# Two token tiles without indexer queries, a turned order of the norm, and weight halves and requests in other places

## What is computed

```python
z = rms_norm(x, g) @ w_in                     # columns split among all heads
qi = rotary(heads(parts[3], 8, 64), pos)      # indexer queries, 512 columns
ki = rotary(heads(parts[4], 1, 64), pos)      # indexer key, 64 columns
wi = parts[5]                                 # 8 head weights
sc = einsum('bqh,bqhs->bqs', wi * IDX_SCALE, relu(einsum('bqhd,bsd->bqhs', qi, ki)))
sc = where(key_pos <= qpos, sc, -inf)
_, sel = top_k(sc, 256)                       # keys that mixer A attends to
```

## Time and profile before

| | us |
|---|---|
| median of 3 runs | 2079.43 |
| lowest and highest run | 2074.18, 2079.83 |
| span of the profiled execution, first to last instruction | 2075.8 |
| TensorE busy in the span | 1955.8 (94%) |
| VectorE, ScalarE, GpSimd busy | 1279.8, 711.6, 682.9 |

### The profile page before, as it was taken

One profiled execution on the slowest core, in us unless ns is written; L12 is line 12 of the kernel. 1 busy time (PEld: TensorE's weight loads), 2 busy tenths in 40 slices (PEclk: granted clock), 3 DMA queues, 4 the chain that ended last, 5 costly groups with the idle time before them and its releaser, 6 DMA issues. The chain is left out here.

```text
span 2075.8 us, 35829 instructions
## 1 busy us (share of the span) xinstructions
PE 1955.8 (94%) x13869; PEld 1778.6 (86%) x13869; DVE 1279.8 (62%) x2449; ACT 711.6 (34%) x1454; POOL 682.9 (33%) x780
## 2 busy tenths in 40 slices
PE   6889999999998897997899988999999999999997
PEld 6867788899997796554599987999999999999997
DVE  5038999997886355443474235786667676643535
ACT  5234322211212473443322145732323232322423
POOL 5757757678890132553300200301010000301000
PEclk9999999999999999999899999899999999999999
DMA  5122232247665633210473020145454532635334
GB/s 171 32 65 74 74 106 86 94 142 229 219 193 168 232 100 95 60 39 27 148 216 110 22 86 28 33 137 184 143 173 139 187 108 77 225 98 175 121 90 139
DMA packets 203741, 251.41 MB, mean 121 GB/s; under 512 B 29172, under 2 KB 184212, under 8 KB 203060
## 3 DMA queue, kind: packets, MB, share of 16 engines
q1 hardware_dynamic: 170980, 167.53, 26.9%
q0 software_dynamic: 9552, 54.95, 7.5%
q10 hardware_dynamic: 23040, 26.63, 3.6%
HBM read 202.38 MB, written 74.00 MB: 133 GB/s over the span
## 5 line engine op out<-in xcount | busy, mean ns | idle before, releaser
L1122 PE MATMUL pz<-w_hi,n_hi 128*128 128x384 f32 (+2 forms) x656 | 225.1, 343 | 3.8 <-DVE n_lo L909 3.6
L1122 PE MATMUL pz<-w_hi,n_lo 128*128 128x384 f32 (+2 forms) x656 | 219.0, 334 | 0.0
L1122 PE MATMUL pz<-w_lo,n_hi 128*128 128x384 f32 (+2 forms) x656 | 218.8, 334 | 0.0
L966 DVE MATCH_REPLACE8 sel<-m,sel 128x1024 f32<-128x1024 f32 (+4 forms) x224 | 205.4, 922 | 0.0
L963 DVE MAX8 m<-sel 128x8 f32<-128x1024 f32 (+4 forms) x224 | 197.6, 925 | 0.1
L3896 PE MATMUL p_c<-n_t_hi,blk 128*128 128x264 f32 x1120 | 191.3, 285 | 1.8 <-DVE blk L3613 1.8
L3896 PEld LDWEIGHTS p_c<-n_t_hi,blk 128*128 128x128 f32 x1120 | 159.0, 188 | 2.0 <-issue 2.0
L1122 PEld LDWEIGHTS pz<-w_hi,n_hi 128*128 128x128 f32 x656 | 126.6, 193 | 23.9 <-issue 18.4
L3896 PE MATMUL p_c<-mix_hi,blk 128*128 128x264 f32 x816 | 141.1, 285 | 0.0
L1128 PE MATMUL pz<-n_hi,w_hi 128*128 128x352 f32 x384 | 126.6, 330 | 5.1 <-ACT z L614 5.1
L3486 POOL DMA_DIRECT2D g_s<-gate x22 | 12.2, 556 | 358.2 <-DVE gate L3701 333.9
(11 more groups left out here) (520 smaller groups left out, 5124.4 us busy)
## 6 DMA issues: line engine op xcount, KB each, us to landing
shared<-in_w_in SPq DMA_DIRECT2D x26, 768.0 KB, 4.7
blk_raw<-in_w_ffn_in SPq DMA_DIRECT2D x72, 256.0 KB, 3.1
relu<-z_qb SPq DMA_DIRECT2D x24, 512.0 KB, 4.9
blk_raw<-in_w_ffn_out SPq DMA_DIRECT2D x58, 192.0 KB, 2.5
z_b<-z ACTq DMA_DIRECT2D x48, 192.0 KB, 1.9
gates<-z ACTq DMA_DIRECT2D x48, 176.0 KB, 2.8
gate<-gates SPq DMA_DIRECT2D x24, 352.0 KB, 3.5
out_new_win_sample<-in_cache_win_kv POOLq DMA_DIRECT2D x8, 1016.0 KB, 5.7
```

Of the source, the lines that this page charges most:

```text
L966: dve.match_replace(out=sel[0:r, o:o + n], in_to_replace=m8[0:r, u, :], in_values=sel[0:r, o:o + n], imm_value=PICKED).then_inc(s_rep, 1)
L1122: m = pe.matmul(out, tokens(a, k, i), b[:, n % 2, k, 0:w], start=(k == 0 and p == 0), stop=(k == KC - 1 and p == 2))
```

## The change

- **Tiles 0 and 1 have no indexer queries.** `UNPICKED` is 2. Block 0 has no step for them (seven steps are left: tiles 2 to 8), and in block 1 their steps compute columns 256 to 328 alone, the key and the head weights (`FIRST_COL`); evacuation, rotation and transpose are narrowed with them.
- **The order of tiles in the norm and in blocks 0 and 1** is 2 to 8, 0, 1 (`X_ORDER`). The rows are loaded, normed and transposed in this order. The first two steps of block 1 (tiles 2 and 3) stand in the loop of the nine head positions and wait there for the high and low part of the eighth and ninth position, which are tiles 0 and 1 (`if s < TILES`). The sample's step has 32 output rows in place of 128.
- **Low halves.** VectorE makes (1, 1) behind its last `normed`, and (2, 0) and (2, 1) behind its last `lo_norm`. GpSimd's (n + 1, 1) of later blocks stands ahead of the seventh rotation of a block in place of the one of tile 6, which is one step earlier from block 2 on.
- **Requests.** SyncE requests (3, 0) and (3, 1) ahead of the sample rows.

```diff
+UNPICKED = TOPK // P
+X_ORDER = list(range(UNPICKED, TILES)) + list(range(UNPICKED))
 for _n in range(len(PROJ)):
-    for _i in range(TILES):
-        if _i < NT or _n < FOLD_FROM:
+    for _k, _i in enumerate(X_ORDER if _n < FOLD_FROM else range(TILES)):
+        if (_i < NT or _n < FOLD_FROM) and (_n or _i >= UNPICKED):
             STEPS.append((_n, _i, None))
-        if _i == FOLD_BEHIND and FOLD_FROM <= _n + 1 < len(PROJ):
+        if _k == FOLD_BEHIND and FOLD_FROM <= _n + 1 < len(PROJ):
             STEPS.append((_n + 1, NT, None))
...
+FIRST_COL = {s: 256 for s, st in enumerate(STEPS) if st[0] == 1 and st[1] < UNPICKED}
...
-        def lows_by_pool(f):
-            return f - (f > 1)
+        low_by_vector = (1, 3, 4, 5)
+
+        def wait_lows(engine, f):
+            by_vector = sum(x < f for x in low_by_vector)
+            if f - by_vector:
+                engine.wait_ge(s_wlo, f - by_vector)
+            if by_vector:
+                engine.wait_ge(s_wlow, by_vector)
...
                 for b in range(2):
                     load_pages(sp, b)
 
+                for j in range(2):
+                    load_half(3, j)
                 last = FIRST_STEP[NIDX] - 1
...
-                for j in range(2):
-                    load_half(3, j)
...
-                    act.activation(z[:, u, 0:w], pz[:, v, 0:w], ACT.Copy).then_inc(s_zev, 1)
+                    c = FIRST_COL.get(s, 0)
+                    act.activation(z[:, u, c:w], pz[:, v, c:w], ACT.Copy).then_inc(s_zev, 1)
...
                 for s in range(FIRST_STEP[len(PROJ)]):
-                    n, i, _ = STEPS[s]
-                    if i == 3:
-                        split_lo(n + 1, 0)
-                    if i == 6:
-                        split_lo(n + 1, 1)
+                    n = BLOCK_OF[s]
+                    k = s - FIRST_STEP[n]
+                    for j in range(2):
+                        if k == (3, 6)[j] and 2 * (n + 1) + j not in low_by_vector:
+                            split_lo(n + 1, j)
                     rotate(s)
...
                 for i in range(1, TILES):
                     lo_norm(i)
                     if i + 2 < TILES:
                         mean(i + 2)
                         normed(i + 2)
+                    if i == 6:
+                        split_lo(1, 1)
+                split_lo(2, 0)
+                split_lo(2, 1)
...
-                    if n == 0:
-                        pe.wait_ge(s_nhi, i + 1)
-                        pe.wait_ge(s_nlo, i + 1)
+                    if s < TILES:
+                        pe.wait_ge(s_nhi, s + 1)
+                        pe.wait_ge(s_nlo, s + 1)
...
-                        out = pz[:, c % 2, 0:w]
+                        c0 = FIRST_COL.get(s, 0)
+                        out = pz[0:rows(i)[1], c % 2, c0:w]
...
-                    for c in range(2 + n):
+                    for c in range(FIRST_COL.get(s, 0) // P, 2 + n):
```

More of the change, by code:

```diff
@@ L373, in rows, with x_place @@
             return (i * P, NS if i == NT else P)
+        def x_place(p):
+            return rows(X_ORDER[p])
         def stores(s):
@@ L430, in x_rows @@
             buf = x_in[:, i % 4, :] if i % 4 < 2 else relu[:, i % 4, :]
-            return buf[0:rows(i)[1], :]
-        def lows_by_pool(f):
-            return f - (f > 1)
+            return buf[0:x_place(i)[1], :]
+        low_by_vector = (1, 3, 4, 5)
[5 more added lines that the diff above has]
+                engine.wait_ge(s_wlow, by_vector)
         with nc.Block() as block:
@@ L439, in load_x @@
                 def load_x(i):
-                    r0, r = rows(i)
+                    r0, r = x_place(i)
                     if i >= 4:
@@ L589, in hi_norm @@
                 def hi_norm(i):
-                    r0, r = rows(i)
+                    r0, r = x_place(i)
                     act.wait_ge(s_xt, i + 1)
-                    if i == NT:
+                    if X_ORDER[i] == NT:
                         for u in range(2):
@@ L691, in _ @@
                     step(i)
-                for s in range(FIRST_STEP[1], FIRST_STEP[NIDX]):
+                for s in range(TILES, FIRST_STEP[NIDX]):
                     step(s)
@@ L827, in rotate @@
                     pool.wait_ge(s_pool, done[0])
-                    add = pool.tensor_tensor(z[:, u, 0:nh * HD], rot[:, 0, 0:nh * HD], rot[:, 1, 0:nh * HD], ALU.add)
+                    add = pool.tensor_tensor(z[:, u, c0:c1], rot[:, 0, c0:c1], rot[:, 1, c0:c1], ALU.add)
                     if COLS[n][0] == "qki":
@@ L912, in lo_norm, with split_lo @@
                     a.then_inc(s_nlo, 1)
[L914 to L917, removed]
+                def split_lo(n, j):
+                    f, w = 2 * n + j, COLS[n][2]
+                    dve.wait_ge(s_whi, f + 1)
+                    dve.tensor_tensor(w_lo[:, n % 2, 4 * j:4 * j + 4, 0:w], w_raw[:, f % RAW, :, 0:w],
+                                      w_hi[:, n % 2, 4 * j:4 * j + 4, 0:w].bitcast(F32), ALU.subtract).then_inc(s_wlow, 1)
                 mean(0)
@@ L1121, in project @@
                             for p, (a, b) in enumerate(((0, w_hi), (1, w_hi), (0, w_lo))):
-                                m = pe.matmul(out, tokens(a, k, i), b[:, n % 2, k, 0:w],
+                                m = pe.matmul(out, tokens(a, k, i), b[:, n % 2, k, c0:w],
                                               start=(k == 0 and p == 0), stop=(k == KC - 1 and p == 2))
```

29 lines of the change are left out of this document (14 added, 15 removed).

## The result

The changed kernel takes 2065.45 us in the median of five runs (2059.37 to 2070.47), beside 2076.59 for the kernel before in the same measurement: ratio 0.9943, 95% interval 0.9922 to 0.9964. A second measurement gave 2068.78 against 2080.45, ratio 0.9940 (0.9917 to 0.9964). That is 11.1 and 11.7 us faster. The profiled execution shows more: its span is 2060.6 us, 15.2 less than before. This difference between the median and the one profile turned out to be the lesson of the case.

The account below looks back on a forecast made before the run. TensorE was taken as the bound, over nine tenths busy, with five early gaps, three followed by low clock. Gains of 8.1 + 2.0 + 6.5 = 16.6 us took 2079.4 to 2062.8 us, bounds 2057.5 to 2067.1, stated range 2056.0 to 2071.0.

Parts of the forecast that it names:

- Head: Up to block 1's start: two block 0 steps and the 2.56 us gap go; gain 8.1 us, bounds 6.9 to 9.5.
- The new wait: Block 1's first steps wait for the last norm tiles' low part behind VectorE's new half; gap about 1.6 us.
- one of my signs of being wrong: Listed refutations: a 72-column step over 3 us, low clock in block 1's first step, a gap before the end's soft-max transposes.
- Block 1: From its first step to block 2's: 0.8 us at the fold, 1.2 from narrow steps; gain 2.0, bounds 0.6 to 5.9.
- The fold gap: Block 1, behind the folded product: TensorE's 3.50 us wait for GpSimd's rotation shrinks to 2.7, slow step kept; gain 0.8 us.
- behind tile 7: Block 1: VectorE's half (2,1) holds the rotation behind the fold, costing 2.0 us against the 1.97 it removes; gain zero.
- Fourth weights: Block 3's folded product: earlier requests save 4.78 us there and 1.71 in the next step; gain 6.5, at least 4.8.
- The port: VectorE and GpSimd lock a shared SBUF port; each VectorE half meeting a rotation stops GpSimd 1.83 us.
- The port did not eat the gain: Rival: all three halves meet rotations, each leaving a gap and slow step; 7.9 us lost, 2070.7 us; chance 0.13.
- the weights came early: Rival denied here: requests held in SyncE's queue past 112 us, so the 6.5 us stay; 2069.3 us; chance 0.06.
- nothing was absorbed at the stage's end: Rival denied here: the VectorE and GpSimd chain doesn't move up, TensorE waits there; up to all lost, 2079 us; chance 0.10.
- the sample rows reached VectorE at 154.39, in time: Rival denied here: weight requests delay the sample rows and VectorE's top-k chain; 2085 us or more; chance 0.04.

Follow-up runs that it names:

- turns_later: Changed kernel, but behind block 1's folded step TensorE turns each tile one step later; project matmuls behind block 2's first dots at 119.9 us, against 125.5.
- still_narrow: Changed kernel with norm waits moved to the steps reading those positions and turns one step later, 72-column steps kept: 2056.70 us against 2079.91 before, ratio 0.9893.
- again: The changed kernel unaltered, profiled a second time; project matmuls behind block 2's first dots at 131.6 us, against 125.5 in its first execution.

## Why the prediction was right, and where not

Forecast 2062.8 us against 2065.45, 16.6 us of gain against 11.1 (11.7 in the second measurement). The sign, the range and the mechanisms held; the gain is some 5 us smaller than the sum, in the main for one reason: the sum counted low clock as if the edits removed it.

- **Head, 8.1 us.** From the end of the seventh step to block 1 the forecast had 3.25 us (48.85 to 52.1); it took 3.42 (46.46 to 49.88). The new wait is 1.52 us, forecast 1.6. Block 1 started 10.3 us earlier, since the seventh step ended 2.4 us earlier: 1.0 at the first wait of the norm and the rest since the low clock behind the earlier trace rows's gap of 2.34 us, which I had not counted, did not come behind the gap of 2.55 (transposes of 1.70 us before, 1.09 here). Neither is the edit's: in the new order the second step starts anywhere from 19.6 to 21.2 us, and this low clock comes in 6 of 11. The step that failed is the clock behind the new wait: I took the earlier trace rows's 1.97 us gap as evidence that it stays high, and it fell to 0.67. The 1.22 us of low clock that the head's gain counted as removed came back one step later, 1.5 us. A low clock there was one of my signs of being wrong.
- **Block 1, 2.0 us.** Measured 1.6 (45.7 to 44.1 us). The fold gap is 2.61 (forecast 2.7), behind tile 7 1.54 (2.0), a narrow step 2.85 (2.7), all close. The slow step that I kept behind the fold did not come; others came at block 1's first step (5.22 us) and at the second narrow step (4.11), which I had not. With the low clock off on both sides block 1 goes from 44.0 to 41.0, 3.0 us: the idle times ahead of turns are 4.94 us where they were 5.81, and both narrow steps save, where I had put the first at nothing.
- **Fourth weights, 6.5 us.** The requests left at 68.9, the wait went, the dots ran at full clock; from block 2's start to M 5.0 us were won, and 1.6 more but for a slow first step of block 2. This term was mis-sized: its sound part is 3.3 to 3.8 us, the waits of 2.81 and 0.83 us in the product. The rest priced the clock of one execution. "At least 4.8" was no bound, since it held the product's slow part.
- **The sum.** At M it was 16.9 us, by the profile almost exact, and that agreement is partly luck: the stretch's clock was 0.95 in this execution, 0.93 before, 0.91 in the next. Taking the low clock out of the terms leaves 8.1 - 1.2 + 2.0 + 3.6 = 12.5 us; the two medians, 11.1 and 11.7, lie a us below, which their intervals allow. The traces give 12.5 too, from the second step to M without the clock, but as 5.9 up to block 1, 3.0 in it and 3.6 behind: one us less in the head and one more in block 1, so the equal total is luck in part as well. Put back one at a time, the steps of block 0, the three halves, the requests and the full steps cost 4.6, 0.5, 3.5 and 2.1 us by the table's last column, between 10 and 11 of the 12.5; no experiment tells what the rest is, which holds what the turned order and the sample step's 32 rows do. The runs' mean granted clock spans the same range in both kernels (0.972 to 0.979 for the changed one, 0.974 to 0.980 for the one before, in the second measurement), so that no lasting clock gain shows.
- **The port.** The rule of the Trainium skill, page "SBUF — State Buffer", section "SBUF: two separate sides", held again: 2.07 and 2.25 us where GpSimd's instructions take 0.73 and 0.87 alone. The price was a little high: a moved half stops GpSimd for 1.3 to 1.4 us, where I had put 1.83, and the gap behind tile 7 is 1.54 and not 2.0. GpSimd's own halves took 3.0 to 3.5 us of its time, but little of that difference reaches TensorE: all three moved halves together are worth 0.5 to 0.9 us at M without the clock, and one stall (the normalisation's) of 2.1 us became a wait of 1.5.
- **Rivals.** The port did not eat the gain, the weights came early, nothing was absorbed at the stage's end (620.25, no gap) and the sample rows reached VectorE at 154.39, in time.

## What to carry over

Price an edit by the idle time and the work it removes, and leave out the low clock that one trace shows behind a gap unless a second execution shows it at the same place; where gaps remained, a slow step that went in one place often turned up behind another gap here. Compare traces at a mark close behind the edit, with the clock of the stretch and the start of the stretch beside it, and leave the verdict on a few us to medians of several runs. Where an engine waits for a result that is one step away, taking the result a step later removed 5.6 us, half as much as the whole change brought.

## What the hardware showed unexpectedly

The low clock doesn't go by the length of a gap: full behind 2.61 and 2.55 us, low behind 1.52 and 0.79 in one execution, and the other way round for the longer ones in the next. At a step with no gap over 0.3 us ahead it was low in `turns_later` and full in `still_narrow`. A trend is there that I can't explain: among the executions in the new order, the gap at 34 us was followed by the low clock in all five that passed the norm's first wait later than 20.4 us and in one of the six that passed it earlier. The late five are also those whose transposes at 16 us ran slowly, 1.20 to 1.91 us against 1.03 or 1.04 in the six, so their late start looks like low clock itself, although the view of granted clock shows 1.00 there. The changed kernel, then `again`:

```profile
16.39 1.03 PE L1070 MATMUL big<-ident,x_in 128*128 128x128 f32 x8
```

```profile
16.57 1.91 PE L1070 MATMUL big<-ident,x_in 128*128 128x128 f32 x8
```

The two kernels with full steps, late waits and later turns held 1.00 up to M.

The Trainium skill, page "TensorE: Matmul & The Clock Gate", section "Part 1: The HAM clock gate (the "warmup" mystery)", says that the gate's watch on TensorE's activity runs free and does not start anew with a kernel, so that the same kernel shows more or fewer slow matmuls at its start from run to run. The transposes above, 1.03 and 1.91 us in one kernel, agree; that the phase decides behind the later gaps too is only argued from the trend, not shown.
